# Gate and up features of six feed-forward networks as 2 by 2 block products, seven of 256 tokens in place of eight, from the third weight pair on

## What is computed

```python
def swiglu(h, w_gu, w_down):
    g, u = jnp.split(h @ w_gu, 2, axis=-1)
    return (jax.nn.silu(g) * u) @ w_down
```

## Time and profile before

| | |
|---|---|
| median of three runs | 3476.19 us |
| lowest and highest | 3475.81, 3477.26 us |
| span of the profiled execution | 3473.2 us |
| own time of the profiled execution | not given; the median is 3.0 us above the span |
| TensorE busy | 3447.0 us, 99% |
| TensorE weight load busy | 2904.9 us, 84% |
| VectorE busy | 1442.7 us, 42% |
| ScalarE busy | 1184.1 us, 34% |
| DMA | 325.49 MB, mean 94 GB/s |
| mean granted clock of TensorE | 0.999 |

### The profile page before, as it was taken

One profiled execution on the slowest core, in us unless ns is written; L12 is line 12 of the kernel. 1 busy time (PEld: TensorE's weight loads), 2 busy tenths in 40 slices (PEclk: granted clock), 3 DMA queues, 4 the chain that ended last, 5 costly groups with the idle time before them and its releaser, 6 DMA issues.

```text
span 3473.2 us, 39367 instructions
## 1 busy us (share of the span) xinstructions
PE 3447.0 (99%) x17361; PEld 2904.9 (84%) x17361; DVE 1442.7 (42%) x1555; ACT 1184.1 (34%) x1754; POOL 154.3 (4%) x133
## 2 busy tenths in 40 slices
PE   9999999999999999999999999999999999999999
PEld 7788888888888888888888888888888888888887
DVE  4554523337744333332336554223422355552333
ACT  3343422236734222232224343222322233532222
POOL 2110000000000000000000220000000000410000
PEclk9999999999999999999999999999999999999999
DMA  5224232222342322233222203222322223023221
GB/s 155 86 78 140 72 110 97 97 79 92 121 146 66 105 96 95 94 109 97 97 97 77 80 28 106 97 97 97 101 97 96 98 78 112 25 73 101 95 99 57
DMA packets 246477, 325.49 MB, mean 94 GB/s; under 512 B 19361, under 2 KB 215505, under 8 KB 246306
## 3 DMA queue, kind: packets, MB, share of 16 engines
q1 hardware_dynamic: 241520, 308.38, 27.1%
q0 software_dynamic: 4784, 14.59, 1.3%
q10 hardware_dynamic: 2, 0.00, 0.0%
HBM read 320.82 MB, written 2.10 MB: 93 GB/s over the span
## 4 chain that ended last, share of the span: by engine, by line
PE 96%; DVE 2%; ACT 2%; issue 0%; POOL 0%; DMA 0%; DVEq 0%; ACTq 0%
PE P L625 28%; PE P L627 28%; PE P L626 28%; PE P L630 3%; PE P L804 3%; PE P L779 3%; PE P L906 1%; DVE BIG L1662 1%; DVE WR L1654 0%; PE P L907 0%; ACT WR L1152 0%; DVE HT L1662 0%; PE P L1081 0%; PE P L783 0%; PE P L1064 0%; DVE STAT L1789 0%
## 5 line engine op out<-in xcount | busy, mean ns | idle before, releaser
L1654 DVE TENSOR_TENSOR WR<-STG,WR 128x2048 fp32r<-128x2048 f32 (+3 forms) x292 | 646.8, 2217 | 1297.5 <-ACT WR L1152 1297.3
L625 PE MATMUL P<-HT,WR 128*128 128x512 f32 (+1 forms) x3008 | 1119.6, 372 | 3.8 <-DVE HT L1662 2.7
L626 PE MATMUL P<-HT,WR 128*128 128x512 f32 (+1 forms) x3008 | 1116.7, 371 | 0.0
L627 PE MATMUL P<-HT,WR 128*128 128x512 f32 (+1 forms) x3008 | 1116.5, 371 | 0.0
L1152 ACT CAST WR<-STG 128x2048 fp32r<-128x2048 f32 (+3 forms) x324 | 558.8, 1726 | 1066.0 <-PE P L627 1065.4
L625 PEld LDWEIGHTS P<-HT,WR 128*128 128x128 f32 x3008 | 567.4, 189 | 102.0 <-DVE HT L1662 3.0
L627 PEld LDWEIGHTS P<-HT,WR 128*128 128x128 f32 x3008 | 567.5, 189 | 97.3
L626 PEld LDWEIGHTS P<-HT,WR 128*128 128x128 f32 x3008 | 567.6, 189 | 96.8
L625 PE MATMUL P<-WR,HT 128*128 128x512 f32 (+1 forms) x1344 | 523.9, 390 | 1.6 <-DVE WR L1654 1.4
L627 PE MATMUL P<-WR,HT 128*128 128x512 f32 (+1 forms) x1344 | 520.7, 387 | 0.0
L626 PE MATMUL P<-WR,HT 128*128 128x512 f32 (+1 forms) x1344 | 520.3, 387 | 0.0
(11 more groups left out here) (204 smaller groups left out, 2413.5 us busy)
## 6 DMA issues: line engine op xcount, KB each, us to landing
STG<-in_w_ffn_gu_dram SPq DMA_DIRECT2D x44, 1024.0 KB, 5.1
STG<-in_ffn_w_gate_dram SPq DMA_DIRECT2D x44, 1024.0 KB, 5.1
STG<-in_ffn_w_up_dram SPq DMA_DIRECT2D x44, 1024.0 KB, 5.1
STG<-in_ffn_w_down_dram SPq DMA_DIRECT2D x44, 1024.0 KB, 4.9
STG<-in_w_ffn_down_dram SPq DMA_DIRECT2D x22, 1024.0 KB, 4.9
STG<-in_w_xkv_dram SPq DMA_DIRECT2D x16, 1024.0 KB, 5.3
STG<-in_w_in_dram SPq DMA_DIRECT2D x12, 1024.0 KB, 5.2
STG<-in_w_xq_dram SPq DMA_DIRECT2D x8, 1024.0 KB, 5.2
```

The source lines that it names most:

```text
L625: pe.matmul(o, lh, rh, start=first, stop=False)
L626: pe.matmul(o, lh, rl, start=False, stop=False)
L627: return pe.matmul(o, ll, rh, start=False, stop=last)
L1654: v.tensor_tensor(rests, src, main.bitcast(F32), ALU.subtract).then_inc(ve.sem, ve.up("lo", n))
```

## The change

Pairs 0 and 1 of each of the six networks stay as they are. For pairs 2 to 10 gate and up are computed together as the 2 by 2 block product [G1 G2; U1 U2] x [X11 X12; X21 X22]. The contraction of 1024 is cut into k 0 to 3 and k 4 to 7 (G1, G2, U1, U2: 512 by 256 each) and the tokens into 0 to 255 and 256 to 511. Seven products of such blocks replace eight:

- combined weights, 128 x 1024 elements each, made on VectorE for every pair: S1 = U1+U2, S3 = G1-U1, S2 = S1-G1, S4 = G2-S2;
- combined tokens, made once for each network: T5 = X12-X11, T7 = X22-X12, T6 = X22-T5, T4 = X21-T6;
- products 1: G1 X11, 2: G2 X21, 3: S4 X22, 4: U2 T4, 5: S1 T5, 6: S2 T6, 7: S3 T7. Each is 2 x 4 x 3 = 24 matmuls of 256 columns.

The sums of products are partly kept in PSUM by going on accumulating (1, 6, 7, 4 in one pair of banks; 5 and 3 in another with 2 beside them) and partly taken by copies: ScalarE copies the banks of 128 x 512 elements after products 1, 6 and 7, VectorE adds product 5 to the copy after 7 ("up"), and products 2 and 5+3 to the other copies ("gate"). Silu is then applied in place on ScalarE to 128 x 1024 elements, and two multiplications on VectorE give the activations.

What was one split of 128 x 2048 per unit is now a split of 128 x 1024 for each of the seven weight forms of a pair, in five slots of WR (and one for T7). The form of product e+5 is made when product e has ended. The order of the products interleaves two pairs: 6, 5, 7, next 1, 4, next 2, 3. The raw weights of two pairs stay in four staging buffers (XN is the fourth). S1 uses BC, so GpSimd's gain transfers are moved behind the form of product 5 of pair 10. The slots of the down operands lie elsewhere, and the first down group takes the token tiles in the order 2, 3, 0, 1, since their banks come free first. The three first down units are split where the last products have freed their slots. Core of the diff, with "..." where lines are left out:

```diff
+FIRST, LAST = 2, 10
+
+
+def products():
+    order = [(FIRST, 1), (FIRST, 2)]
+    for i in range(FIRST, LAST + 1):
+        order += [(i, 6), (i, 5), (i, 7)] + [(i + 1, 1)] * (i < LAST) + [(i, 4)] + [(i + 1, 2)] * (i < LAST) + [(i, 3)]
+    return order
+
+
+PRODUCTS = products()
+PLACE = {ip: e for e, ip in enumerate(PRODUCTS)}
+NFORM = 5
...
+        def stage_free(n):
+
+            s, part, i = (*units[n][0], 0)[:3]
+            m = raw(n)
+            if m is not None and m == 3:
+                return [ve.at(s, "act", 2 * FIRST - 1)]
+            if m is not None and m >= 4:
+                return [ve.at(s, "form", PLACE[i - 2, 3 if part == "g" else 4])]
+            if m is not None:
+                n0 = U[s, "g", 0] + 1 + m
+                return [ac.at("hi", n0), low(n0)]
+            if n in downs or n - 1 in downs or n - 2 in downs:
+                s = units[n][0][0]
+                last = ((LAST - 1, 3), (LAST, 3), (LAST, 4))[i // 2]
+                return [ve.at(s, "form", PLACE[last])]
+            return [ac.at("hi", n - NSTG), low(n - NSTG)]
...
+        def form(s, e):
+            return form_slot(s, (e + 3) % NFORM)
+
+        def form_free(s, e):
+
+            return mm.at(s, "form", e - NFORM) if e >= NFORM else mm.at("w", U[s, "g", 0] + (1, 1, 2, 3, 3)[e])
+
+        def weights_of(s, i, p):
+
+            gate, up = (staged(U[s, part, i]) for part in ("g", "u"))
+            return {1: gate[:, 0:1024], 2: gate[:, 1024:2048], 3: gate[:, 1024:2048], 4: up[:, 1024:2048],
+                    5: BC[:, i % 2, :], 6: gate[:, 0:1024], 7: up[:, 0:1024]}[p]
+
+        def tokens_of(s, p):
+
+            rows = lambda ap: ap.rearrange("p (k n) -> p k n", k=4)
+            return [{1: HT[:, z, 0:4, 0:256], 2: HT[:, z, 4:8, 0:256], 3: HT[:, z, 4:8, 256:512], 4: HT[:, z, 0:4, 256:512],
+                     5: rows(RB[:, 1024 * z:1024 * z + 1024]), 6: rows(RB[:, 2048 + 1024 * z:3072 + 1024 * z]),
+                     7: rows(form_slot(s, NFORM)[z])}[p] for z in range(2)]
...
+                for e, (i, p) in enumerate(PRODUCTS):
+                    sums, rest = 4 * (i % 2), 4 * (i % 2) + 2
+                    if p == 1:
+                        for j in range(2):
+                            room(sums + j, (ve, (s, "act", 2 * i + 1)))
+                    if p == 2:
+                        for j in range(2):
+                            room(rest + j, (ve, (s, "gate", i)))
+                    if p == 6:
+                        g.wait_ge(*ac.at(s, "kept", i, 1))
+                    if p == 7:
+                        g.wait_ge(*ac.at(s, "kept", i, 6))
+                    if p == 4:
+                        g.wait_ge(*ac.at(s, "kept", i, 7))
+                    if p == 3:
+                        g.wait_ge(*ve.at(s, "up", i))
+                    if p in (4, 5, 6, 7):
+                        g.wait_ge(*ve.at(s, "T", p))
+                    g.wait_ge(*ve.at(s, "form", e))
+                    w = [z.rearrange("p (k n) -> p k n", k=4) for z in form(s, e)]
+                    x = tokens_of(s, p)
+                    for j in range(2):
+                        o = {1: P[:, sums + j, 0:256], 2: P[:, rest + j, 0:256], 6: P[:, sums + j, 0:256],
+                             5: P[:, rest + j, 256:512], 7: P[:, sums + j, 0:256], 4: P[:, sums + j, 0:256],
+                             3: P[:, rest + j, 256:512]}[p]
+                        for k in range(4):
+                            lh, ll = (z[:, k, 128 * j:128 * j + 128] for z in w)
+                            pe.matmul(o, lh, x[0][:, k], start=k == 0 and p in (1, 2, 5), stop=False, skip_group_check=True)
+                            pe.matmul(o, lh, x[1][:, k], start=False, stop=False, skip_group_check=True)
+                            last = pe.matmul(o, ll, x[0][:, k], start=False, stop=k == 3, skip_group_check=True)
+                    last.then_inc(mm.sem, mm.up(s, "form", e))
+                out_proj(s, 22, lambda k, t: (slot_tile(0, k, t), slot_tile(1, k, t)), lambda k, t: ve.at(s, "slot", k),
+                         [2, 3, 0, 1])
...
+                for e, (i, p) in enumerate(PRODUCTS):
+                    sums = P[:, 4 * (i % 2):4 * (i % 2) + 2, 0:256]
+                    pair = ACTS[:, 2 * i:2 * i + 2, :]
+                    if p in (1, 6, 7):
+                        g.wait_ge(*mm.at(s, "form", e))
+                        if p == 7:
+                            g.wait_ge(*ve.at(s, "act", 2 * i - 1))
+                        a.copy(UP2 if p == 7 else pair[:, :, 0:256] if p == 1 else pair[:, :, 256:512], sums).then_inc(
+                            ac.sem, ac.up(s, "kept", i, p))
+                    if e + NFORM < len(PRODUCTS):
+                        main(e + NFORM)
+                    if p == 3:
+                        g.wait_ge(*ve.at(s, "gate", i))
+                        fn(pair, pair, ACT.Silu, s, "silu", i)
+                    if (i, p) == (LAST, 2):
+                        for k in range(4):
+                            prepare(k)
+                    if (i, p) == (LAST, 7):
+                        hi(U[s, "d", 0])
+                        for k in range(4, 8):
+                            prepare(k)
                 a.preload_act_table_set("natural_log_exp_and_others")
-                for k in range(4, 8):
-                    prepare(k)
-                after((s, "u", 10))
+                hi(U[s, "d", 2])
+                hi(U[s, "d", 4])
...
+                def token_sums():
+                    first, second, up_first, up_second = T32
+                    g.wait_ge(*ve.now())
+                    quadrant(0, 1)
+                    quadrant(1, 4)
+                    g.wait_ge(*ve.now())
+                    tt(first, second, first, ALU.subtract, s, "T32", 5)
+                    quadrant(3, 3)
+                    g.wait_ge(*ve.now())
+                    tt(second, up_second, second, ALU.subtract, s, "T32", 7)
+                    g.wait_ge(*ve.now())
+                    tt(up_second, up_second, first, ALU.subtract, s, "T32", 6)
+                    quadrant(2, 2)
+                    g.wait_ge(*ve.now())
+                    tt(up_first, up_first, up_second, ALU.subtract, s, "T32", 4)
...
+                def s1_s3(i):
+                    gate, up = U[s, "g", i], U[s, "u", i]
+                    for n in (gate, up):
+                        g.wait_ge(*landed[stage_of(n)].at("unit", n))
+                    if i >= FIRST + 2:
+                        g.wait_ge(*ve.at(s, "form", PLACE[i - 2, 5]))
+                    else:
+                        g.wait_ge(*ve.now())
+                    low_, high = staged(up)[:, 0:1024], staged(up)[:, 1024:2048]
+                    tt(BC[:, i % 2, :], low_, high, ALU.add, s, "S1", i)
+                    g.wait_ge(*ve.at(s, "S1", i))
+                    tt(low_, staged(gate)[:, 0:1024], low_, ALU.subtract, s, "S3", i)
+
+                def s2(i):
+                    low_ = staged(U[s, "g", i])[:, 0:1024]
+                    g.wait_ge(*ve.at(s, "S3", i))
+                    g.wait_ge(*ve.at(s, "form", PLACE[i, 1]))
+                    tt(low_, BC[:, i % 2, :], low_, ALU.subtract, s, "S2", i)
+
+                def s4(i):
+                    both = staged(U[s, "g", i])
+                    g.wait_ge(*ve.at(s, "S2", i))
+                    g.wait_ge(*ve.at(s, "form", PLACE[i, 2]))
+                    tt(both[:, 1024:2048], both[:, 1024:2048], both[:, 0:1024], ALU.subtract, s, "S4", i)
...
+                token_sums()
+                after((s, "g", 0))
+                activated(0)
+                tokens(5)
+                tokens(6)
+                s1_s3(FIRST)
+                rests(0)
+                s2(FIRST)
+                rests(1)
+                s4(FIRST)
+                tokens(7)
+                rests(2)
+                activated(1)
+                rests(3)
+                rests(4)
+                tokens(4)
+                for e, (i, p) in enumerate(PRODUCTS):
+                    sums, others = 4 * (i % 2), 4 * (i % 2) + 2
+                    pair = ACTS[:, 2 * i:2 * i + 2, :]
+                    if p == 7:
+                        g.wait_ge(*mm.at(s, "form", e))
+                        g.wait_ge(*ac.at(s, "kept", i, 7))
+                        tt(UP2, UP2, P[:, others:others + 2, 256:512], ALU.add, s, "up", i)
+                    if p == 3:
+                        g.wait_ge(*mm.at(s, "form", e))
+                        tt(pair, pair, P[:, others:others + 2, :], ALU.add, s, "gate", i)
+                    if e + NFORM < len(PRODUCTS):
+                        rests(e + NFORM)
+                    if p == 3:
+                        g.wait_ge(*ac.at(s, "silu", i))
+                        stt(pair[:, :, 0:256], pair[:, :, 0:256], scale, P[:, sums:sums + 2, 0:256], ALU.mult, ALU.mult)
+                        stt(pair[:, :, 256:512], pair[:, :, 256:512], scale, UP2, ALU.mult, ALU.mult, s, "act", 2 * i)
```

(70 more changed lines are left out.)

124 lines of the change are left out of this document (73 added, 51 removed).

## The result

The changed kernel takes 3395.98 us (median of four runs, 3395.77 to 3396.12); the kernel before took 3476.65 in the runs beside it. The ratio is 0.9768, 95% interval 0.9755 to 0.9782: 81 us faster. The prediction was 3396 us (3396.3 at the end of its sum).

What follows compares the result with a forecast made beforehand. TensorE, busy for 99% of the span, was taken as the bound. 3473.2 - 87.3 + 5.4 + 2 = 3393.3 us of span, plus 3.0 us carried over to the median, gave 3396.3 us; range 3386 to 3430.

Steps and rivals of the forecast that it cites:

- TensorE's work: Pairs 2 to 10: 168 matmuls of 256 columns replace 96 of 512, 1.62 us less a pair, 87.3 us less.
- The upper bound: Start of each product: if every one restarted at 0.20 us instead of 0.12, 30 us would be given back.
- The rule of the Trainium skill: TensorE's matmul step of N/2.4 + 2.5 ns: 2.37 us less a pair, 128 us in all; set aside for measured steps.
- The other rule of that page: Weight loads overlap matmuls only in differing row groups: a pair 35.9 us after, 30.7 before, a loss; rejected from the trace.
- VectorE's cover: VectorE's work per pair, 16.8 us in 20.1 (83%), stays hidden behind TensorE; thinnest slack 0.6 us.
- The chain: Each pair: VectorE's S1, S3 and gate sum, ScalarE's Silu and copy after product 6, then TensorE; slack 0.6 us.
- rival B: Short TensorE gaps in each pair, 0.5 us each: 3423 us, chance 0.20; larger gaps, 3434 to 3470, 0.07 more.
- The transfers: Gate and up weights for pair i+2: up lands at 1.9 and is used at 2.6, hidden with 0.7 us.
- Rival C: Up weights land late for S1 in pairs 4 to 10, idling TensorE: 101 us, 3497 us; chance 0.05.
- The beginning of a network: VectorE's extra token sums, rests and first forms, 28 us before product 1 of pair 2, cost nothing.
- The end of the products: Pair 10, between products 7 and 4: TensorE idles 0.9 us for ScalarE's copy, 5.4 us more over six networks.
- The entry of down: First down group waits for banks after pair 10's activations: slack 0.4 us, 0.3 us a network taken, 2 us more.

## Why the prediction was right

**TensorE's work.** Right. A pair takes 20.16 us, predicted 20.14, and 21.76 before, so 54 x 1.60 = 86.4 us instead of 87.3. The pace of the earlier trace rows, taken where a network begins, held for 1464 matmuls in a row in each network, and the run with eight short products gave it independently. The upper bound, 30 us for a restart at every product, came to nothing: a restart costs 0.1 us only where TensorE really waited. Nor does a new operand cost a step of 0.20 us, as the prediction had it: every product begins on new operands, at 0.12 us where nothing is waited for. The rule of the Trainium skill (TensorE: Matmul & The Clock Gate, Back-to-back issue gap), by which the change would have given 128 us, is given there for a single matmul by itself, and it does not describe this stream: 0.12 us a step against its 0.109, in the changed kernel too. The other rule of that page, on weight loads beside matmuls, stands there under The mechanism, in the part on packing small matmuls, and it does not hold here either: a load and a matmul of all rows fit into every 0.12 us. The prediction's 35.9 and 30.7 us for it are not the load added to the measured steps, as it says; that estimate would be 38.1 and 32.0 us, with the same conclusion.

**VectorE's cover.** Right in place and in cost, a little short in size. VectorE was busy for 15.9 us a pair, predicted 16.8, since operations that follow each other without a wait start every 1.14 us. The chain gained about 0.2 us by this and 0.1 on ScalarE, whose copy starts 0.97 us after the Silu, and its slack was 0.9 us and not 0.6. One reading was wrong, without a place in the sum: the kernel before has two activations a pair on VectorE (132 for 66 pairs in the earlier trace rows), not four, so VectorE had 6.0 us a pair, 27% and not the 34% that rival B starts from. That this chain is the one that matters was shown by four runs: work on it costs at once, the same work beside it costs nothing, and turning two ScalarE operations round takes most of it off TensorE's path.

**The transfers.** Right: up landed 9.4 us after the first issue, as worked out, and 1.3 us ahead of its use (0.7 predicted). The prediction named a wait of VectorE for a transfer ahead of S1 as a sign of being wrong. There are four, 2.2 us in all, but for pair 3, where the chain does not stand; in the 42 pairs that it meant there is none. Rival C, the slower end, is real as a mechanism: four forms later the kernel is 6% slower than before. I priced it at one microsecond for each late one; waits of 4.5 us cost half as much again, through the clock.

**The beginning of a network.** Nothing, as predicted: no wait in the list stands there.

**The end of the products.** The gap was predicted at 0.9 us a network and measured at 0.83 + 0.10. The entry of down was sized at 0.3 us a network within 0 to 1; it cost nothing, with 1.2 us of slack where I had seen 0.4.

**The sum.** Pairs -86.4, gaps +5.6, down 0. The remaining 1.7 us of span are lost in the first 25 us of the run. There the first gain landed 0.8 us later than in the profile before (3.1 us of wait against 2.3), and the slow steps of the start (0.21 us for 256 columns) went on to 19.7 us instead of 17.2. Neither is taken for an effect of the change: the first wait is 2.1 to 2.3 us in three kernels with the change and 3.1 to 3.3 in the others, and 3.3 in the kernel before with eight short products. -86.4 + 5.6 + 1.7 = -79.1, the measured difference of the spans. Against the predicted span of 3393.3 us the misses are +0.9, +0.2, -2 and +1.7, together +0.8; and the median lies 1.9 us above the span where 3.0 had been carried over. That the median came within 0.3 us of the sum is luck of this offsetting; the main term by itself was right within 0.9 us.

## What to carry to other kernels

When one engine is the bound, price a change by the start-to-start step of the very shape that the new work will have, and look for that shape in the old trace: seven eighths of the columns were worth 86 us and not 147, because two short matmuls cost 0.24 us where a long one cost 0.227. For the engines that hide the rest, a mean load says little. Follow each hand-over through every in-order queue it stands in; here a copy of 0.6 us behind a Silu decided, and its order cost nothing to change. And where work is moved to cover one gap, look at what it covered before.

## What the runs showed of the hardware that was not expected

- After TensorE had stood for 4.1 us, in six places, its clock was granted at 0.50 (1.2 GHz) and 7 to 14 matmuls of 512 columns took steps of 0.43 us, 1.5 to 3.0 us lost beside the wait. With 42 waits of 4.5 us the mean clock was 0.96 and 94 us were lost beyond the waits. Shorter waits mostly left the clock at 1.00, but the length of the wait alone does not tell: of 42 waits of 1.1 to 2.5 us one, of 1.75 us, was followed by slow steps, and six longer ones were not.
- VectorE starts one 128x1024 operation every 1.14 us where none waits on the one before, and every 1.25 where it does, with a shown duration of 1.22 in both cases.
- In a stream of 256 columns a wait of TensorE costs 0.26 us more than the idle time in the view of waits: 0.16 from the modelled end, 0.10 in the first step after it. A delay under 0.16 us is in no view of waits at all.
